# Layer 1 of a hybrid decoder step: indexer first, scores of the sampled sequences kept in SBUF, prompt attention and its output projection moved ahead of the sample softmax

## The reference

```python
q, k, v, qi, ki, wi, din, bg, cg = split_cols(rms_norm(x) @ w_in, [512, 128, 128, 256, 64, 4, 512, 512, 512])
q, k  = rope(rms_norm(q)), rope(rms_norm(k))         # 8 query heads, 2 key heads of 64
qi, ki = rope(qi), rope(layer_norm(ki))              # indexer: 4 heads of 64, one key of 64
sc = einsum(relu(qi . ki_all), wi)                   # a score for each (query, key)
idx = top_k(where(causal, sc, NEG), k)               # prompt: 64 of 256; samples: 256 of 2048 cached + 8 new keys
att = softmax(q . k[idx] / 8) @ v[idx]               # over the chosen keys only
d = bg * causal_conv3(cg * din)                      # short gated convolution
x = x + concat(att, d) @ w_out                       # 1024 x 1024
```

## Time and profile before

| | us |
|---|---|
| median of 3 runs (lowest, highest) | 1918.65 (1917.32, 1920.63) |
| the profiled execution: its own time | 1925.65 |
| its span, first to last instruction | 1924.0 |
| PE busy / DVE busy / ACT busy | 1743.1 / 1193.6 / 825.9 |
| span of layer 1's mixer (634.9 to 1034.9) | 400.0 |
| experts after it (1034.9 to 1924.0) | 889.1 |

### The profile page before, as it was taken

The page is one execution under the profiler, slowest core; times in us unless marked ns, Lnnn a source line. Parts: engine busy times, 40 slices in busy tenths (PEclk is TensorE's granted clock), DMA queues, the critical chain, the costliest instruction groups (busy, mean ns, idle before and its releaser), DMA issues.

```text
span 1924.0 us, 22099 instructions
## 1 busy us (share of the span) xinstructions
PE 1743.1 (91%) x8266; PEld 1326.2 (69%) x8266; DVE 1193.6 (62%) x1494; ACT 825.9 (43%) x855; POOL 181.9 (9%) x214
## 2 busy tenths in 40 slices
PE   5999999699999887838897999999998999999995
PEld 4665645498997455535664888778887888778883
DVE  1795434444443143995103888968886888778883
ACT  1114230233331122044202577656766767566771
POOL 3005701000000041162100000000000000000000
PEclk9998699899999988858978999999999999999997
DMA  8323012655543121152502699979997999789991
GB/s 270 129 88 95 1 55 66 219 169 180 180 135 132 44 65 33 36 145 63 171 4 98 235 339 393 320 275 320 386 318 280 354 355 364 281 328 323 383 327 65
DMA packets 174470, 385.84 MB, mean 201 GB/s; under 512 B 30598, under 2 KB 77831, under 8 KB 174234
## 3 DMA queue, kind: packets, MB, share of 16 engines
q1 hardware_dynamic: 166674, 367.78, 54.5%
q0 software_dynamic: 7696, 16.69, 3.1%
HBM read 377.55 MB, written 7.19 MB: 200 GB/s over the span
## 4 chain that ended last, share of the span: by engine, by line
PE 83%; DVE 9%; ACT 5%; issue 1%; POOL 1%; DMA 1%; POOLq 0%; ACTq 0%; DVEq 0%
PE psum L1268 74%; PE psum L1755 2%; DVE zone L2419 1%; ACT parts L1201 1%; DVE zone L2418 1%; PE psum L1868 1%; PE psum L1429 1%; ACT arena L902 1%; PE psum L1427 1%; DVE parts L2539 1%; PE psum L1473 1%; DMA arena<-state_conv_b 1%; PE psum L1744 1%; DVE arena L2583 1%; ACT zone L898 0%
## 5 line engine op out<-in xcount | busy, mean ns | idle before, releaser
L1268 PE MATMUL psum<-parts 128*128 128x512 f32 (+3 forms) x5100 | 1047.6, 367 | 32.5 <-DVE parts L2226 8.4
L1268 PEld LDWEIGHTS psum<-parts 128*128 128x128 f32 (+1 forms) x5100 | 872.9, 188 | 195.8 <-issue 18.5
L2539 DVE TENSOR_TENSOR parts<-arena,parts 128x2048 fp32r<-128x2048 f32 (+1 forms) x280 | 604.0, 2168 | 128.3 <-ACT parts L1201 127.0
L1201 ACT ACTIVATE parts<-arena 128x2048 fp32r<-128x2048 f32 (+1 forms) x280 | 509.8, 1822 | 248.0 <-PE psum L1268 242.1
L1268 PE MATMUL psum<-arena 128*128 128x320 f32 (+10 forms) x1264 | 309.6, 405 | 5.5 <-DVE arena L2352 1.8
L1268 PEld LDWEIGHTS psum<-arena 128*128 128x128 f32 (+3 forms) x1264 | 204.5, 199 | 110.3 <-issue 61.1
L1268 PE MATMUL psum<-arena,zone 128*128 128x512 f32 (+5 forms) x390 | 137.6, 518 | 6.1 <-ACT zone L1042 2.6
L1268 PEld LDWEIGHTS psum<-arena,zone 128*128 128x128 f32 (+3 forms) x390 | 65.9, 198 | 69.8 <-issue 63.2
L1069 ACT ACTIVATE parts<-arena 128x1024 fp32r<-128x1024 f32 x66 | 67.4, 1058 | 107.8 <-PE psum L1268 107.8
L902 ACT ACTIVATE zone<-psum 128x512 f32<-128x512 f32 (+11 forms) x81 | 34.4, 467 | 160.7 <-PE psum L1268 67.3
L2226 DVE TENSOR_TENSOR parts<-arena,parts 128x1024 fp32r<-128x1024 f32 x66 | 78.6, 1223 | 32.7 <-ACT parts L1069 32.7
(11 more groups left out here) (356 smaller groups left out, 1008.7 us busy)
## 6 DMA issues: line engine op xcount, KB each, us to landing
arena<-o_we_down SPq DMA_DIRECT2D x88, 1024.0 KB, 5.4
arena<-o_we_gate SPq DMA_DIRECT2D x64, 1024.0 KB, 6.6
arena<-o_we_up SPq DMA_DIRECT2D x64, 1024.0 KB, 5.6
arena<-o_we_gate SPq DMA_DIRECT2D x32, 768.0 KB, 4.3
arena<-o_we_up SPq DMA_DIRECT2D x32, 768.0 KB, 4.3
arena<-e_w_in SPq DMA_DIRECT2D x7, 2048.0 KB, 18.2
arena<-e_w_gate SPq DMA_DIRECT2D x11, 1024.0 KB, 5.5
arena<-e_w_up SPq DMA_DIRECT2D x11, 1024.0 KB, 8.1
```

The source lines that it names most:

```text
L1201: act.activation(hi_piece(i, words), raw_piece(i, words), ACT.Copy).then_inc(behind("piece_hi"), 1)
L1268: return pe.matmul(dst, w, m, start=start, stop=stop)
L2539: dve.tensor_tensor(lo_piece(i, words), raw_piece(i, words), hi_piece(i, words).bitcast(F32), ALU.subtract).then_inc(behind("piece_lo"), 1)
```

## The change

- The indexer's columns (768 to 1091 of the weight, 324) are projected first, then k and v (256). q, `din`, `cg` and `bg` are projected after the indexer's sums, while DVE searches.
- The 64 indexer-key transposes are done in two blocks, half before the norm and half while DVE rotates, into the pages' own places. The dots become one block: all upper halves of four sequences, then all lower halves.
- `choose_halves` gets three more inserts: the squares' sums of q and k, their normalisation and rotation, and the packing of the sample queries.
- The raw scores of all four pairs are computed during the search and copied from PSUM to SBUF (`s_kept`); afterwards the bias product stands alone in PSUM, and DVE adds the two (`mask_scores`).
- The prompt rows of the output projection, and the half of the sample rows that comes from the convolution, run before and between the sample softmax. After the last values only 8 matmuls are left.
- Loads of key pages, value pages, w_out and the first expert pieces get other places and other conditions on SP and POOL.

The core of the diff:

```diff
+            turn_kidx(range(4))
             norm(2)
...
+            token_major(0, (0, 1, 2), (None, None, None))
+            token_major(5, KV, (None, None, (sem("tok_ready"), 1)))
+            pe.wait_ge(sem("halo1_ready"), 1)
+            turn_kidx(range(4, NB))
...
+            for g in range(2):
+                for odd in range(2):
+                    if g:
+                        pe.wait_ge(sem("relu_s_ready"), odd + 1)
+                    for b in range(4 * g, 4 * g + 4):
+                        r0, h0 = 32 * (b % 4), 64 * odd
+                        for a in range(NPG // 2):
+                            ins = mm(bank(2 * odd + a // 4)[r0:r0 + 32, P * (a % 4):P * (a % 4) + P], qi_b[h0:h0 + 64, b, :],
+                                     kidxT[b][h0:h0 + 64, a, :], True, True)
...
+            token_major(1, (0, 1, 2), (None, None, None))
+            channels(2, DIN, "din_mm", lambda c: reached("work_s_ready"))
+            channels(3, 0, "cg_mm", lambda c: (sem("din_ready"), 1) if c == 3 else (sem("tok_ready"), 7 + c))
...
+            turn_keys(3)
+            pe.wait_ge(sem("s_p_taken"), 1)
+            pe.wait_ge(sem("tails1_ready"), 2)
+            scores(2)
+            turn_prompt(0)
+            turn_keys(1)
+            scores(3)
+            pe.wait_ge(sem("s_kept"), 2)
+            scores_prompt(1)
+            turn_keys(0)
+            pe.wait_ge(sem("s_p_taken"), 2)
+            scores(1)
+            turn_prompt(1)
+            scores(0)
...
+            mask(0)
+            out_part(1, 0, 6, (0, 1))
+            turn_pair(0)
+            mask(1)
+            pe.wait_ge(sem("pt_ready"), 4)
+            out_part(1, 1, 6, (0, 1))
+            turn_pair(1)
+            mask(2)
+            weigh_pair(0)
+            turn_pair(2)
+            mask(3)
+            weigh_pair(1)
+            turn_pair(3)
+            weigh_pair(2)
+            weigh_pair(3)
...
-            choose_halves({8: short_conv, 12: conv_gate, 14: lambda: prompt_max(0), 16: lambda: prompt_probs(0),
-                           22: lambda: prompt_max(1), 24: lambda: prompt_probs(1)})
+            choose_halves({8: qk_sums, 12: qk_rotate, 14: short_conv, 17: pack_queries, 19: conv_gate,
+                           21: lambda: prompt_max(0), 23: lambda: prompt_probs(0), 27: lambda: prompt_max(1), 29: lambda: prompt_probs(1)})
             join_halves()
...
+                own.mark(dve.tensor_tensor(p[:, 0:PAST], s_kept[q], psum[:, 0:PAST], ALU.add))
+                own.mark(dve.tensor_tensor(p[:, PAST:], s_new[q], bank(4)[:, 0:NT], ALU.add))
+                own.wait()
+                own.link(dve.reduce_max(mx[:, 0:1], p, AX))
...
+            mask_scores(0)
+            add_out(5, 1, 0, 6)
+            share(0)
+            mask_scores(1)
+            add_out(6, 1, 1, 6)
+            share(1)
+            mask_scores(2)
+            attended(0)
+            share(2)
+            mask_scores(3)
+            attended(1)
+            share(3)
+            attended(2)
+            attended(3)
+            for h in range(2):
+                add_out(7 + h, 2, h, 4 + h)
```

ScalarE's order changes with it; what matters later is that it copies the kept scores between the prompt's two steps:

```diff
+            turn_keys(3)
+            exp_prompt(0)
+            keep_scores(2)
+            turn_prompt(0)
+            turn_keys(1)
+            keep_scores(3)
+            turn_keys(0)
+            exp_prompt(1)
+            keep_scores(1)
+            turn_prompt(1)
+            keep_scores(0)
```

More of the change, by code:

```diff
@@ L394, in step_program @@
         v_new = new(NB, P)
-        q_blk = new(NB, 64)
+        where[0] += NB * 64
         WORK = where[0]
+        MIX1 = FREE + 10 * T
         half_s = new(HALF)
@@ L411, in step_program @@
         ki_s, ki_v, ki_ms, ki_rs = new(3), new(3), new(3), new(3)
-        rope_t = [at(WORK + 240 * i, 3, 10, 8) for i in range(4)]
+        rope_t = [at(MIX1 + 240 * i, 3, 10, 8) for i in range(4)]
+        s_new = [new(NT) for _ in range(NB // 2)]
         v_tok = new(3, P)
@@ new lines, in _ @@
+            act.wait_ge(sem("rotT_mm"), 4)
+            copy(kkT[:, 1, :], bank(7)[:, 0:T], "rotT_ready")
+            act.wait_ge(*reached("wsT_mm"))
+            act.activation(ws, bank(2, 2, NS), ACT.Copy).then_inc(*reaches("ws_ready"))
+            for i in range(2):
+                act.wait_ge(sem("idx_p_mm"), i + 1)
+                if i:
+                    act.wait_ge(sem("sc_p_ready"), 1)
+                act.activation(relu_p.rearrange("p a b -> p (a b)"), psum[:, 512 * (3 + 2 * i):512 * (5 + 2 * i)],
+                               ACT.Relu).then_inc(sem("relu_p_ready"), 1)
@@ L1114, in _ @@
+            for i, t0, n in TILES:
+                act.wait_ge(sem("tok_mm"), i + 7)
+                copy(tok[0:n, i, 0:512], bank(i)[0:n, :], "tok_ready")
+            act.wait_ge(sem("tok_ready"), 9)
+            act.wait_ge(*reached("isum_mm"))
+            act.activation(squares1, tok[:, :, 0:640], ACT.Square).then_inc(*reaches("qk_squared"))
             act.wait_ge(*reached("din_free"))
@@ new lines, in turn_keys, with keep_scores @@
+            def turn_keys(q):
+                for b in (2 * q, 2 * q + 1):
+                    for g in range(4):
+                        act.wait_ge(sem("kT_mm"), 8 * PAIRS.index(q) + 4 * (b % 2) + g + 1)
+                        copy(k_T[b][:, 512 * g:512 * g + 512], bank(TURN2[g % 2]), "kT_ready")
+            def keep_scores(q):
+                act.wait_ge(sem("scores_mm"), PAIRS.index(q) + 1)
+                act.activation(s_new[q], bank(7)[:, 0:NT], ACT.Copy)
+                copy(s_kept[q], psum[:, 0:PAST], "s_kept")
@@ new lines, in _ @@
+            pe.wait_ge(sem("relu_p_ready"), 2)
+            for g in range(2):
+                pe.wait_ge(sem("relu_s_ready"), 2 * g + 2)
+                for u, lo, w in KEY_PARTS:
+                    k0 = PAST // 2 * u + lo
+                    ins = pe.matmul(psum[NS * u:NS * u + NS, 512 * 5 + lo:512 * 5 + lo + w], ws[:, g, :], relu_s[g][:, k0:k0 + w],
+                                    start=g == 0, stop=g == 1, skip_group_check=True)
+            ins.then_inc(*reaches("isum_mm"))
+            token_major(1, (0, 1, 2), (None, None, None))
@@ L1766, in mask, with turn_pair @@
                 ins.then_inc(sem("masked_mm"), 1)
[L1768 to L1779 removed]
+            def turn_pair(q):
```

665 lines of the change are left out of this document (347 added, 318 removed).

## The result

The changed kernel takes 1854.96 us (median of 4 runs, 1854.13 to 1859.42) against 1919.64 of the kernel before, a ratio of 0.966 (95% interval 0.963 to 0.969): 65 us faster, where 20 were forecast. The profiled execution spans 1857.8 us.

The account below looks back on a forecast made before the run. The prediction took PE's list, not DVE's search, to end the search's stage. Its stages summed to -64 + 48 - 4 = -20 us: profiled 1905.5, median 1898, range 1864 to 1918.

Parts of the forecast that it names:

- First stage: Mixer up to the first MAX8: 134 to about 70 us, -64, with 26 us for the indexer dots.
- second rival: First stage: the indexer dots run at the low clock, 29.5 us through the whole chain, median 1927; chance .14.
- Search's stage: First MAX8 to the sample softmax: 122.5 to about 170 us, +48.
- the second tile's scores 5.6, at the low clock after the gap: Search's stage: prompt scores after the second keeping of scores, priced at 5.6 us.
- what ends the stage is PE, not the search: Search's stage: PE's list runs to about 875, while DVE's search and join end at 862.
- VectorE's idle time: Search's stage: DVE waits 27 us for the second prompt tile's scores, at no further cost.
- first softmax at 875: End of the search's stage: PE finishes its scores and the first sample softmax comes at 875.
- Last stage: Sample softmax and projection: 143.3 to about 140 us, -4, the mixer ending at 1014.4.
- four value products of two sequences, 4 x 15.4: Last stage: all four pairs' value products run at 1.2 GHz, 61.6 us.
- the clock stays up or comes back: Last stage, rival: value products keep or regain full clock, median 1860 to 1878; chance .19.
- first case: Last stage: clock back after some 5.5 us in each value product, about 10.8 each, mixer end near 994, median 1878.
- rival of the handovers: Search's stage: ten PE and ACT handovers cost 1.5 to 2.5 us more each, time stays about 1919; chance .07.

Follow-up runs that it names:

- first: The changed kernel with neighbouring indexer dots on alternating halves of the partitions; median 1847.8 us, ratio to the kernel before 0.960.
- third experiment: The changed kernel with indexer dots alternating both partition halves and column groups; median 1850.1 us, ratio to the kernel before 0.961.
- second experiment: The changed kernel with the dots' two inner loops swapped, so neighbours write alternating groups of 32 output partitions; median 1849.0 us, ratio to the kernel before 0.961.
- fourth experiment: The changed kernel with ten more MAX8 on VectorE behind the search's last round, ahead of the joining of the halves; 1856.2 us.
- ninth: The changed kernel with q's projection again ahead of the indexer's dots instead of behind their sums; 1878.9 us.
- fifth experiment: The changed kernel with 12 unread matmuls filling TensorE's idle times before the last pairs' transposes and value products; 1843.6 us.
- tenth: The changed kernel with dots on alternating halves, a reordered last stage, last values loaded in two steps, convolution projection in the second handover; 1825.4 us.
- thirteenth: The tenth with VectorE's work placed earlier in the search and two unread matmuls between the last two pairs' value products; 1809.5 us.
- twelfth: The ninth with VectorE's other work three rounds earlier in the search, up to the first prompt tile's reciprocal; 1860.7 us.

## Why the prediction was wrong

The direction was right, the size a third of what was measured, and the time lies 9 us under the range. The step that failed is the price of TensorE's clock: work behind idle time was counted at 1.2 GHz to its end, in the search's stage and in the value products, and ran in large part at 2.4. By the prediction's own steps, in the profile's times:

| | forecast | measured | difference |
|---|---|---|---|
| start of the first projection | 634.9 | 631.9 | -3.0 |
| to the first MAX8 | 70.1 | 65.3 | -4.8 |
| to the end of the scores | 170 | 154.7 | -15.3 |
| to the last residual add | 139.4 | 119.5 | -19.9 |
| experts | 889.1 | 886.4 | -2.7 |

- **First stage: right, a little too dear.** The block of dots came at 22.1 us instead of 26, for .17 a dot instead of .213. That it lost the overlap that the kernel before had is shown by the first and third experiment. The second rival (dots at the low clock) did not come: 1.00 throughout; it came in the profile of the second experiment, behind the same waits.
- **Search's stage: the step that failed is the clock after the handovers.** I put "the second tile's scores 5.6, at the low clock after the gap", keys 7.6, scores 9.3, and turns and values 9.9. They took 2.96, 5.2, 6.35 and 7.65: with the first tile's values (3.35 for 5.3) that is 12 of the 15 us. I had priced values, scores and turns from rows of the kernel before that stood behind long waits (14.59, and these of 7.63 and 13.61 us), and let the clock stay down:

```profile
813.28 5.62 PE L1268 MATMUL psum<-zone 64*128 64x256 f32 x16 [7.63 <-DVE zone L2383]
...
859.42 3.77 PE L1723 MATMUL psum<-arena,zone 128*128 128x128 f32 x16 [13.61 <-ACT zone L1157]
863.88 5.64 PE L1268 MATMUL psum<-arena,zone 128*64 128x128 f32 x32 [0.69 <-ACT arena L902]
```

The prediction's own spoke against that: behind the values of 4.97 the second tile's scores took 2.96, full speed. Here the clock was back after the turns behind each wait of 5.21, and the 2.03 ahead of the second tile's scores had not cost it. Up to the first handover my list was right to about a microsecond (98 us from 694.3, forecast 97).
- **That "what ends the stage is PE, not the search" was half right.** VectorE's idle time is near the forecast (27 us forecast, 20.22 measured), and the bias is there before the scores end (862 and 875 forecast, 848 and 852 measured). It lies 24 us ahead of its use, because 20 us of projection stand between; the forecast's own list has that too, so its "first softmax at 875" was too early by its own count. But the fourth experiment shows only some 7 us of slack for VectorE's list, and the ninth shows that the search's beginning has none. I had looked at VectorE only at its last wait, not at the places where PE waits for it.
- **Last stage: the step that failed is "four value products of two sequences, 4 x 15.4".** Two took 8.2, one 15.3, one 14.3: 16 of the 20 us. I took the clock of one stretch for a rule. The row said that it can stay down for 15 us, not that it must; the third pair's products began at full clock right behind turns at half clock (938.00). That the idle time in front has a part in losing the clock there is shown by the fifth experiment, as the forecast had it; why two pairs got it back and two did not stays open.
- **The rival "the clock stays up or comes back"** is what happened, in part: of its two cases (1878, 1860) neither; the rival looked at the last stage alone, and with the 15 us of the search's stage, the start and the first stage the time went below both. Its first case put the last stage at 119 us (875 to 994), and 119.5 were measured, but by chance: not four products at 10.8, but two at 8.2 and two near 15. I gave it .19, with the Trainium skill's rule (TensorE: Matmul & The Clock Gate, Part 1, "What's actually happening") that "activity releases the throttle" beside it, and held one row against it. The rows of the search's stage now agree with the rule, two pairs of value products do not (20.4 us at 0.50 from 911.10).
- The rival of the handovers did not come (5.21 and 2.03, where 5.5 and 2.2 were counted). Key pages, value pages and POOL hid where I had put them; the waits before transposes were 2.18 to 2.46, as counted.

## What to carry to other kernels

A clock that one stretch kept low is one sample: price a stretch behind idle time at both levels, and for many stretches count neither all at the worst nor all at the best. Where one engine's long loop carries small work for another, ask at each insert who waits for it; the loop's end may have slack while its beginning has none. When a delay costs nothing in the total, look whether it was slack or whether another term moved the other way. Filling a wait needs work whose data are there: the cheap fillings here were reordering of bias products, and in one place two matmuls that nobody reads.

## What the runs showed of the hardware that I had not expected

- Small products overlap along both dimensions of the array: 128 dots of 64 rows by 32 columns took 22.1 us with neighbours in the same part, 8.3 with alternating halves, 4.2 of work with alternating halves and column groups. The Trainium skill (TensorEngine Tiling (Array Packing), Tiling Modes, Key Properties) says that tiles work independently; the prediction drew on it for halves alone.
- Behind 0.99 us without work between two value products the clock fell in the changed kernel and in the tenth, and the 11 to 13 us of the same products that followed did not bring it back; two matmuls in that time kept it in the fifth and the thirteenth. Yet 0.99 us ahead of the scores at 785.92 left it at full.
- The same list behind the same waits ran at either level in different executions: the prompt's indexer scores 3.72 and 7.17 us behind 0.40 (changed kernel and second experiment), the second tile's scores 2.96 and 5.55 behind 2.04 (twelfth and ninth).
